# First mixer: one VectorE operation per block for gate differences and mask, ahead of the exponentials of the rows

## The reference

```python
q = l2_norm(heads(q, GDN_DK)); k = l2_norm(heads(k, GDN_DK))    # q, k, v after a causal convolution and silu
g = -exp(a_log) * softplus(a_raw + dt_bias)                      # one gate per token and head
g_cum = jnp.cumsum(g.reshape(b_, h_, n, CHUNK), axis=-1)
incl = idx[:, None] >= idx[None, :]
decay = jnp.exp(jnp.where(incl, g_cum[..., :, None] - g_cum[..., None, :], -jnp.inf))
a_low = jnp.where(strict, jnp.einsum('bhncd,bhnsd->bhncs', k_beta, k) * decay, 0.0)
sol = lax.linalg.triangular_solve(eye + a_low, rhs, left_side=True, lower=True, unit_diagonal=True)
attn_intra = jnp.einsum('bhncd,bhnsd->bhncs', q, k) * decay
q_decay = q * jnp.exp(g_cum)[..., None]
```

## Time and profile before

| | us |
|---|---|
| median of the runs shown (3 runs) | 2417.15 |
| lowest and highest | 2416.0 and 2418.23 |
| the profiled execution | 2417.23 |
| its span | 2415.4 |

### The profile page before, as it was taken

How to read it: one execution, slowest core, us unless ns; L and a number is a source line. 1 busy time by engine, 2 the same in 40 slices (tenths; PEclk the granted TensorE clock), 3 DMA queues, 4 the chain that set the end, 5 groups by cost and what they waited for, 6 DMA issues and landing times.

```text
span 2415.4 us, 29293 instructions
## 1 busy us (share of the span) xinstructions
PE 2292.1 (95%) x11250; PEld 1859.9 (77%) x11250; DVE 1127.7 (47%) x1381; ACT 895.8 (37%) x1185; POOL 366.7 (15%) x335
## 2 busy tenths in 40 slices
PE   3899999979999999999899999999999999999998
PEld 2677777767888888797678888887887887888886
DVE  2455555544444432335454443235656664656522
ACT  2333333333323221546532222225655663444411
POOL 4122222232000001000130000110000015222211
PEclk9999999989999999999999999999999999999999
DMA  5111011101232222221022222232111113223221
GB/s 181 52 36 35 35 35 35 35 18 71 87 104 89 102 89 103 72 96 43 18 90 102 93 98 96 96 140 88 53 66 66 66 53 105 97 94 103 88 98 59
DMA packets 30003, 186.42 MB, mean 77 GB/s; under 512 B 3024, under 2 KB 5200, under 8 KB 9312
## 3 DMA queue, kind: packets, MB, share of 16 engines
q1 hardware_dynamic: 27904, 177.64, 21.5%
q0 software_dynamic: 2016, 7.60, 0.9%
HBM read 181.01 MB, written 7.37 MB: 78 GB/s over the span
## 4 chain that ended last, share of the span: by engine, by line
PE 85%; DVE 6%; ACT 4%; issue 2%; POOL 1%; DMA 0%; DVEq 0%; POOLq 0%; ACTq 0%
PE ps L1556 23%; PE ps L1558 23%; PE ps L1557 23%; PE ps L1716 2%; PE ps L1726 2%; PE ps L1729 2%; DVE convd L974 2%; PE ps L2151 1%; PE ps L2094 1%; PE ps L2134 1%; PE ps L1908 1%; PE ps L2161 1%; DVE wl L818 1%; PE ps L1946 1%; DVE convd L971 1%
## 5 line engine op out<-in xcount | busy, mean ns | idle before, releaser
L1556 PE MATMUL ps<-xh,wh 128*128 128x512 f32 x1888 | 771.9, 409 | 9.9 <-DVE wl L818 6.7
L1558 PE MATMUL ps<-xh,wl 128*128 128x512 f32 x1888 | 739.9, 392 | 0.0
L1557 PE MATMUL ps<-xl,wh 128*128 128x512 f32 x1888 | 738.8, 391 | 0.0
L818 DVE TENSOR_TENSOR wl<-raw,wh 128x2048 fp32r<-128x2048 f32 x161 | 381.9, 2372 | 337.8 <-ACT wh L329 337.8
L329 ACT ACTIVATE wh<-raw 128x2048 fp32r<-128x2048 f32 x161 | 307.9, 1913 | 584.6 <-PE ps L1558 571.9
L1556 PEld LDWEIGHTS ps<-xh,wh 128*128 128x128 f32 x1888 | 357.4, 189 | 92.3 <-issue 17.9
L1558 PEld LDWEIGHTS ps<-xh,wl 128*128 128x128 f32 x1888 | 356.4, 189 | 76.0
L1557 PEld LDWEIGHTS ps<-xl,wh 128*128 128x128 f32 x1888 | 357.6, 189 | 70.2 <-issue 6.2
L1556 PE MATMUL ps<-hid_h,wh 128*128 128x512 f32 x528 | 208.6, 395 | 0.0
L1558 PE MATMUL ps<-hid_h,wl 128*128 128x512 f32 x528 | 208.6, 395 | 0.0
L1557 PE MATMUL ps<-hid_l,wh 128*128 128x512 f32 x528 | 208.6, 395 | 0.0
(11 more groups left out here) (322 smaller groups left out, 2898.0 us busy)
## 6 DMA issues: line engine op xcount, KB each, us to landing
raw<-in_stream SPq DMA_DIRECT2D x161, 1024.0 KB, 5.0
hankd<-tabd SPq DMA_DIRECT2D x1, 3072.0 KB, 17.7
hank<-hankd POOLq DMA_DIRECT2D x4, 768.0 KB, 5.0
hT<-in_xT SPq DMA_DIRECT2D x1, 2048.0 KB, 8.5
keepd<-hT POOLq DMA_DIRECT2D x1, 2048.0 KB, 10.2
hT<-keepd POOLq DMA_DIRECT2D x8, 256.0 KB, 4.9
out<-hT SPq DMA_DIRECT2D x8, 256.0 KB, 2.1
mats<-in_mats SPq DMA_DIRECT2D x1, 896.0 KB, 10.1
```

The costliest lines, as they stand in the source:

```text
L818: dve.tensor_tensor(wl[:, s, :], raw[:, s, :], wh[:, s, :].bitcast(F32), ALU.subtract).then_inc(lo_made, 1)
L1556: pe.matmul(out, w_hi, a_hi, start=start, stop=False)
L1557: pe.matmul(out, w_hi, a_lo, start=False, stop=False)
L1558: return pe.matmul(out, w_lo, a_hi, start=False, stop=stop)
```

## The change

VectorE no longer waits for `eg_made`. The subtraction and the minimum over all four blocks become one scalar_tensor_tensor per block: bank 6 minus the block's gate column (a pointer scalar), then the minimum with `cap`. ScalarE takes eG behind DT instead of ahead of E. The semaphore `e_sub` goes; TensorE waits for `e_min` in its place before it writes bank 6 again. The second mixer's `oag_made`, which was `e_sub` under another name, becomes a semaphore of its own and counts from zero.

```diff
@@ ScalarE, head
                         act.wait_ge(rows_done, h + 1)
-                        act.activation(eG[:, :], ps[:, 6, :], ACT.Exp).then_inc(eg_made, 1)
                         act.wait_ge(e_min, h + 1)
                         act.activation(DT[:, :, :], E[:, :, :], ACT.Exp).then_inc(dt_made, 1)
+                        act.activation(eG[:, :], ps[:, 6, :], ACT.Exp).then_inc(eg_made, 1)
                         evac_vz(p, h)
@@ VectorE, head
                         dve.wait_ge(rows_done, h + 1)
-                        dve.wait_ge(eg_made, h + 1)
-                        dve.tensor_tensor(E[:, :, :], bank(6), col(0), ALU.subtract).then_inc(e_sub, 1)
-                        dve.wait_ge(e_sub, h + 1)
-                        dve.tensor_tensor(E[:, :, :], E[:, :, :], mat("cap").unsqueeze(1).to_broadcast([P, TT, P]), ALU.min).then_inc(e_min, 1)
+                        for c in range(TT):
+                            e = dve.scalar_tensor_tensor(E[:, c, :], ps[:, 6, c * P:(c + 1) * P], hcol[:, p, 0, c:c + 1], mat("cap"), ALU.subtract, ALU.min)
+                        e.then_inc(e_min, 1)
                         conv_v(p, h)
@@ GpSimd, second mixer
                 pool.wait_ge(ob_made, AGAIN + n + 1)
-                pool.wait_ge(oag_made, AGAIN + n + 1)
+                pool.wait_ge(oag_made, n + 1)
@@ TensorE, chain step 4
                     pe.wait_ge(eg_made, h + 1)
-                    pe.wait_ge(e_sub, h + 1)
+                    pe.wait_ge(e_min, h + 1)
```

More of the change, by code:

```diff
@@ L249, in build @@
                              "ba_rows", "ba_cols", "ba_beta")]
-        (conv_step, qk_silu, vz_silu, qk_sq, ss_done, rqk_ln, rqk_made, qkn_made, picked, rows_done, eg_made, e_sub, e_min,
+        (conv_step, qk_silu, vz_silu, qk_sq, ss_done, rqk_ln, rqk_made, qkn_made, picked, rows_done, eg_made, oag_made, e_min,
          dt_made, tb_made, kk_done, attn_qk_done, at_made, attn_made, qd_made, kt_done, vt_done, kdkbe_made, vb_made,
@@ L255, in build @@
                 "conv_step", "qk_silu", "vz_silu", "qk_sq", "ss_done", "rqk_ln", "rqk_made", "qkn_made", "picked",
-                "rows_done", "eg_made", "e_sub", "e_min", "dt_made", "tb_made", "kk_done", "attn_qk_done", "at_made",
+                "rows_done", "eg_made", "oag_made", "e_min", "dt_made", "tb_made", "kk_done", "attn_qk_done", "at_made",
                 "attn_made", "qd_made", "kt_done", "vt_done", "kdkbe_made", "vb_made", "am_made", "amt_done", "t_made",
@@ L275, in build @@
         final_made, cw_made = [sem(n) for n in ("final_made", "cw_made")]
-        (qw_hi, qr_val, qr_hi, qr_lo, sx_made, den_made, rinv_made, oag_made, oa_made, ob_made,
+        (qw_hi, qr_val, qr_hi, qr_lo, sx_made, den_made, rinv_made, oa_made, ob_made,
          half_filled, latent_done, kr_hi, kr_lo, kb_hi, nsink_made, pv_done, tr_done, pt_act, pt_dve,
          sc_done, qw_lo, kb_val, rcol_done, rcol_made) = (
-            ss_done, rqk_ln, rqk_made, qkn_made, picked, rows_done, eg_made, e_sub, e_min, dt_made,
+            ss_done, rqk_ln, rqk_made, qkn_made, picked, rows_done, eg_made, e_min, dt_made,
             tb_made, kk_done, attn_qk_done, at_made, attn_made, qd_made, kt_done, vt_done, kdkbe_made, vb_made,
```

## The result

| | us | ratio to the kernel before |
|---|---|---|
| before, same chip | 2416.22 (2416.0 to 2418.23) | |
| the changed kernel, six runs | 2402.05 (2401.35 to 2406.42) | 0.9945 [0.9933, 0.9957] |
| its profiled execution (span 2404.4) | 2406.18 | |
| forecast (range) | 2407.0 (2403.5 to 2411.5) | |

The account below looks back on a forecast made before the run. The prediction took each head's front to be bound by VectorE's in-order instructions. An earlier convolution would save 1.28 us in each of 8 heads, 10.2 us in all: 2417.2 - 10.2 = 2407.0 us, range 2403.5 to 2411.5.

Parts of the forecast that it names:

- What bounds the front: Each first-mixer head's front is bound by VectorE's in-order instructions; starting the convolution earlier starts everything behind it earlier.
- Removed: the wait for eG: VectorE starts on the rows matmul directly, 0.12 us behind its end, at 161.26, without 0.70 us waiting for eG.
- Replaced: Four 128-column operations on E instead of two of 512, 0.26 us apart; convolution at 162.30, gain 1.28 us a head.
- rival of short operations that don't overlap: Four operations on E take their full 0.346 us each; gain only 0.94 us a head, 2409.7 us; 10%.
- Moved: eG behind DT on ScalarE costs nothing: table load keeps 0.45 us of cover, k transposes 1.33 us, qd 1.7 us.
- rival of qd holding up the convolution: GpSimd's qd beside a convolution step costs 0.39 us; gain 0.89 us a head, 2410.1 us; 5%.
- Sum: Eight heads at 1.28 us each give 10.2 us; 2417.2 - 10.2 = 2407.0 us.
- "perhaps" of 4%: Rival of a larger gain: low bound of the pitch (12.2 us), perhaps one half-clock stretch fewer; 2404 us; 4%.
- the clock rival: Half-clock stretches shift into every head's dense part, losing 1.7 us each; slower, 2420.6 us; 5%.
- The range: 2403.5 to 2411.5 us: holds the forecast, two reduced gains, most of the larger; leaves out no change and slower.

Follow-up runs that it names:

- delay_full: The changed kernel with three VectorE operations on scratch tiles added between the last operation on E and the convolution in every head; 2415.74 us.
- conv_first: The changed kernel with three of the four convolution steps of v moved ahead of the four operations on E; 2392.1 us.
- order_only: The kernel before with eG behind DT and no VectorE wait for eG; subtraction and minimum stay two operations of 512 columns; 2407.97 us.
- before_fill: The kernel before with small extra matmuls, results unread, in TensorE's gaps of the last head; 2412.76 us.
- again_g: The changed kernel, unchanged, one more profiled run, the fastest of a series of six; 2401.92 us.

## Why the prediction was right or wrong

- *What bounds the front* was right: delay_full gives the time back by the start of the convolution alone, and conv_first gains by bringing it forward once more.
- *Removed: the wait for eG.* Here a term was mis-sized. I took 0.12 us for VectorE to follow TensorE, from T's start at 179.31; the timeline shows 0.04 (0.02 in the chain, 216.79 to 216.82). Those 0.08 us are the difference between 1.28 and the measured 1.36 us a head: 0.7 us of the sum. T was the wrong row to take it from: it stands behind two waits inside the hardware loop, and in the last two heads, which are written out, the same T follows L1726 by 0.04 us (last section). The nearer row would have been eG's own start, 0.02 us behind the same rows matmul.
- *Replaced:* right. 0.26 us a pitch, 343 ns alone against 346 from L1055. The rival of short operations that don't overlap is out: they start 0.08 us before the one ahead ends, four in a row. The Trainium skill (VectorE: DVE Perf Modes, the section on the TRN2 errata) is right that the fixed part is paid by each operation: 343 ns for a quarter of the columns against 748 for the long form. The formula's 291 ns, an estimate from that page, was too low for this operation and the overlap more than made up for it.
- *Moved:* right. The table load kept 0.53 us of cover (0.45 predicted), the k transposes didn't wait, L1700 lost its idle time, and qd cost the convolution nothing (751 ns at most). The rival of qd holding up the convolution is out. That the minimum's 1.07 us was qd beside two operands in SBUF is now shown by order_only's 0.69; the Trainium skill (SBUF — State Buffer, Who interferes with whom) has it so.
- *Sum.* 8 x 1.36 = 10.9 us by the measured front; with it the forecast would have been 2406.3 us. The step that failed is that the front was taken for the whole sum: time at half clock was put at nothing, except as a rival on the slow side and as a "perhaps" of 4% on the other. The last head gained 2.0 to 3.7 us instead of 1.28, of which 0.6 to 2.3 are its time at half clock. What lies behind the mixer differs by 3.2 us between profiles of the changed kernel with the half-clock stretches in it. And a half-clock stretch behind L1715 does cost 1.33 us, as the clock rival had it (1.7 assumed), but in none to three of seven heads, not in every one. That rival also read the stretch at 111.20 as costing next to nothing; it cost 0.5 us.
- *The range* was made of sizes of the front's gain alone and has no term for the spread between runs of one kernel, 2.2 us in the three runs of before and 6.8 us in 17 of the changed kernel. The median of the 17 lies inside it, 2.3 us below the forecast. That the median of the first six lies below it comes from four of the six being near 2402 us; of the eleven others two were (2401.81 and 2401.92). What decides where the half-clock stretches fall in a run stays open. As far as the runs show it was luck that so many of the first six were short; a difference between chips is not ruled out.
- *Open* are also 0.57 us between w and norm that the changed kernel's heads no longer lose (15.27 us in all heads). Before, the second, fourth and sixth heads took 15.61, 15.39 and 15.38 us, in before_fill likewise. It isn't the front that takes them away: delay_full has a front as long as before and 15.26 to 15.27 us in all heads.

## What to carry to other kernels

Where an in-order engine bounds a stage, ask of each wait in its queue whether the work behind it needs it: here VectorE waited for an exponential that it didn't read, and taking that wait away, which also moved qd out of the minimum's way, carried four fifths of the front's gain. Then look for the engine's idle time just ahead of the wait that remains, and move independent work there: conv_first gained more than the change did. And before giving a range to a gain of half a per cent, look at where the granted clock is at half in the trace: a stretch of it costs nothing where enough waiting follows and over a microsecond in dense work, and a change that shifts the waits changes which it is; one that uses the waits up, as conv_first does, pays 1.6 us for a stretch that cost 0.04 before.

## What the runs showed of the hardware that was not expected

- A half-clock stretch of 3.4 us cost 0.04 us when it began 2.5 us behind the rows (again_g), 0.4 to 0.5 us in the kernel before at 10.2 to 10.4 us behind them, 1.33 at 11.4 to 11.7, and 1.6 us at 2.5 us in conv_first, where TensorE has no waits left behind it.
- Extra matmuls without use made the last head shorter, 44.81 instead of 47.08 us, by raising its granted clock from 0.85 to 0.92; in the kernel before 45.70 instead of 50.74 us (0.80 to 1.00). In the gaps of the dense heads alone they gained nothing.
- VectorE, standing still with one wait ahead of E, started 0.04 us behind the modelled end of the rows matmul in all eight heads. T stands behind two waits, the second on a count that VectorE itself had raised before. In the six heads of the hardware loop it started 0.12 to 0.13 us behind the end of L1726, in the two written-out heads 0.04. Why the loop and the second wait together cost 0.09 us is not shown. The lines of the kernel before, in its second head (T follows at 179.31) and its seventh:

```profile
178.03 1.16 PE L1726 MATMUL ps<-X,TI 128*128 128x128 f32 x8
...
468.21 1.16 PE L1726 MATMUL ps<-X,TI 128*128 128x128 f32 x8
...
469.40 0.69 DVE L1042 TENSOR_TENSOR T<-T,ps 128x512 f32<-128x512 f32 x1 [2.74 <-PE ps L1726]
```
